# The start of a two-block layer: weight unit 1 in halves, and another order of the first norm's work

## The reference

```python
def rms_norm(x, g):
    y = x * lax.rsqrt(jnp.mean(x * x, axis=-1, keepdims=True) + NORM_EPS)
    return y * g

h = rms_norm(x, norm_mix_g[l])
proj = h @ w_in[l]                       # 1024 -> 5120
q, k, v, c_b, c_c, c_u, g_a, g_b = jnp.split(proj, IN_SPLITS, axis=-1)
q = rms_norm(q.reshape(B, S, SB_HEADS, SB_HEAD_DIM), q_norm_g[l])   # likewise k
branch_a = stick_breaking_attention(q, k, v) @ w_sb_branch[l]
branch_b = short_conv_mixer(c_b, c_c, c_u, conv_w[l]) @ w_conv_branch[l]
merged = jax.nn.sigmoid(g_a) * branch_a + jax.nn.sigmoid(g_b) * branch_b
x = x + merged @ w_out[l]
x = x + hierarchical_moe(rms_norm(x, norm_ffn_g[l]), ...)  # 32 experts
# second block: attention, a gated unit, and a SwiGLU network
```

## Time and profile before

| | before |
|---|---|
| three executions, us | 715.24, 716.45, 718.52 |
| the profiled execution, us | 715.94 |
| its span, first to last instruction, us | 714.1 |
| TensorE busy | 650.1 us, 91% |
| VectorE, ScalarE, GpSimd busy | 47%, 36%, 4% |
| mean granted TensorE clock | 0.959 |
| moved by the transfers | 186.06 MB, mean 261 GB/s |

### The profile page before, as it was taken

One profiled execution on the slowest core, in us unless ns is written; L12 is line 12 of the kernel. 1 busy time (PEld: TensorE's weight loads), 2 busy tenths in 40 slices (PEclk: granted clock), 3 DMA queues, 4 the chain that ended last, 5 costly groups with the idle time before them and its releaser, 6 DMA issues.

```text
span 714.1 us, 11499 instructions
## 1 busy us (share of the span) xinstructions
PE 650.1 (91%) x4957; PEld 530.3 (74%) x4957; DVE 333.6 (47%) x409; ACT 260.5 (36%) x323; POOL 30.4 (4%) x19
## 2 busy tenths in 40 slices
PE   6999999999989999669787899999899999999995
PEld 5789999999856555244432587778689999999994
DVE  5864437566461222001010465759846444444446
ACT  5747454453411111101010453766236443333330
POOL 0610000000100000000000000330000000000000
PEclk9999999999999999957977899999999999999998
DMA  8979334787999999999999998335445556750001
GB/s 316 408 205 357 121 130 167 253 304 262 406 382 406 386 406 408 409 406 406 409 409 407 389 407 315 116 106 189 143 152 177 177 182 191 259 193 0 0 1 60
DMA packets 108491, 186.06 MB, mean 261 GB/s; under 512 B 9632, under 2 KB 33312, under 8 KB 108448
## 3 DMA queue, kind: packets, MB, share of 16 engines
q1 hardware_dynamic: 108160, 185.36, 70.8%
q10 hardware_dynamic: 288, 0.07, 0.0%
HBM read 184.37 MB, written 1.05 MB: 260 GB/s over the span
## 4 chain that ended last, share of the span: by engine, by line
PE 74%; DMA 11%; DVE 10%; ACT 2%; issue 2%; SPq 1%; DVEq 0%; ACTq 0%
PE ps L656 18%; PE ps L658 17%; PE ps L657 17%; PE ps L936 6%; DMA ring<-in_w_up_e 5%; DMA ring<-in_w_down_e 4%; PE ps L956 4%; PE ps L902 3%; DVE w_lo L1767 3%; DMA ring<-in_w_in 1%; PE ps L964 1%; PE ps L966 1%; PE ps L785 1%; ACT w_hi L1303 1%; DVE X L2314 1%
## 5 line engine op out<-in xcount | busy, mean ns | idle before, releaser
L1303 ACT ACTIVATE w_hi<-ring 128x2048 fp32r<-128x2048 f32 (+1 forms) x77 | 141.1, 1859 | 5.4 <-DMA ring<-in_w_in 5.2
L1767 DVE TENSOR_TENSOR w_lo<-ring,w_hi 128x2048 fp32r<-128x2048 f32 x49 | 114.8, 2354 | 52.2 <-ACT w_hi L1303 52.1
L656 PE MATMUL ps<-xT_hi,w_hi 128*128 128x256 f32 x320 | 90.6, 283 | 0.0
L658 PE MATMUL ps<-xT_hi,w_lo 128*128 128x256 f32 x320 | 90.6, 283 | 0.0
L657 PE MATMUL ps<-xT_lo,w_hi 128*128 128x256 f32 x320 | 90.6, 283 | 0.0
L936 PE MATMUL ps<-ring,heT 128*32 128x256 f32 x880 | 59.0, 409 | 15.6 <-DMA ring<-in_w_up_e 11.0
L656 PE MATMUL ps<-hT_hi,w_hi 128*128 128x256 f32 x224 | 64.0, 286 | 0.0
L657 PE MATMUL ps<-hT_lo,w_hi 128*128 128x256 f32 x224 | 63.4, 283 | 0.0
L658 PE MATMUL ps<-hT_hi,w_lo 128*128 128x256 f32 x224 | 63.3, 283 | 0.0
L657 PEld LDWEIGHTS ps<-xT_lo,w_hi 128*128 128x128 f32 x320 | 61.4, 192 | 0.4
L656 PEld LDWEIGHTS ps<-xT_hi,w_hi 128*128 128x128 f32 x320 | 61.4, 192 | 0.4
(11 more groups left out here) (315 smaller groups left out, 1128.5 us busy)
## 6 DMA issues: line engine op xcount, KB each, us to landing
ring<-in_w_in SPq DMA_DIRECT2D x29, 1024.0 KB, 13.7
ring<-in_w_up_e SPq DMA_DIRECT2D x28, 1024.0 KB, 13.4
ring<-in_w_gate_e SPq DMA_DIRECT2D x27, 1024.0 KB, 12.4
ring<-in_w_down_e SPq DMA_DIRECT2D x26, 1024.0 KB, 13.4
ring<-in_w_gate SPq DMA_DIRECT2D x11, 1024.0 KB, 5.4
ring<-in_w_up SPq DMA_DIRECT2D x11, 1024.0 KB, 5.5
ring<-in_w_down SPq DMA_DIRECT2D x11, 1024.0 KB, 5.0
ring<-in_w_out SPq DMA_DIRECT2D x8, 1024.0 KB, 9.8
```

Of the source, the lines that this page charges most:

```text
L656: mm(o, a_hi, b_hi, start=start, stop=False, skip_group_check=True)
L658: return mm(o, a_lo, b_hi, start=False, stop=stop, skip_group_check=True)
L1303: return nc.scalar.activation(o, i, ACT.Copy)
L1767: tt(w_lo[slot][:], ring[:, slot, :], f32(w_hi[:, i % WB, :]), ALU.subtract).then_inc(lo_made, 1)
```

## The change

Five edits are made together. Their names in the diff:

1. Unit 1 is loaded by two transfers of 512 KB, with a semaphore each (`land_w1`, `land[1]`), and split in halves on ScalarE and VectorE (`split_upper(1, j)`, `split_lower(1, j)`). TensorE starts on it when the first lower half is made, and waits for the second at its third step. SyncE issues one more transfer, ahead of the constants and of unit 2.
2. The norm's gain gets its own semaphore (`land_g1`). TensorE's first transposes wait for the identity matrix and x alone.
3. ScalarE splits unit 2 (`hi(2)`) ahead of the second token tile's statistics; VectorE's `lo(2)` stands ahead of the second `refine`, so ahead of `diag`.
4. `first_norm_row` stands between the two token tiles of unit 2, and no longer between units 1 and 2.
5. ScalarE's squares for K come ahead of `hi(4)` and of the copy to `y1_row`, which is now inside `qk_square(0)`, behind `hi(4)`. VectorE's `lo(4)` stands inside `qk_norm(0)`, between the reduction and the small steps.

```diff
@@ SyncE
                 if i >= RING:
                     sp.wait_ge(unit_used, i - RING + 1)
-                if i > 0:
+                if i == 1:
+                    for j in range(2):
+                        sp.dma_start(ring[:, 1, :].rearrange("p (k n) -> p k n", k=KU)[:, 2 * j:2 * j + 2, :],
+                                     src[:, 2 * j:2 * j + 2, :]).then_inc((land_w1, land[1])[j], 16)
+                if i > 1:
                     sp.dma_start(ring[:, slot, :].rearrange("p (k n) -> p k n", k=KU), src).then_inc(land[slot], 16)
@@ TensorE
-                pe.wait_ge(*((part_lo, 1) if i == 0 else (lo_made, i + 1)))
+                pe.wait_ge(*((part_lo, i + 1) if i < 2 else (lo_made, i + 1)))
...
-                        if (i, t, kk) == (0, 0, 2):
-                            pe.wait_ge(lo_made, 1)
+                        if i < 2 and (t, kk) == (0, 2):
+                            pe.wait_ge(lo_made, i + 1)
...
-            pe.wait_ge(land_id, 16 * 2)
+            pe.wait_ge(land_id, 16)
...
-                               (split_made, SP_H + 2 * i + 1, SP_H + 2 * i + 2) if i < 2 else None)
+                               (split_made, SP_H + 2 * i + 1, SP_H + 2 * i + 2) if i < 2 else None,
+                               first_norm_row if i == 2 else None)
...
             proj(1, False)
-            first_norm_row()
             proj(2, False)
@@ ScalarE
-            act.dma_start(g1, norm_mix_g[0].rearrange("(p k) -> p k", k=KD)).then_inc(land_id, 16)
+            act.dma_start(g1, norm_mix_g[0].rearrange("(p k) -> p k", k=KD)).then_inc(land_g1, 16)
...
-            first_unit(0)
+            split_upper(0, 0)
             hR_copy(0)
-            first_unit(1)
+            split_upper(0, 1)
             hR_copy(2)
-            hi(1)
+            split_upper(1, 0)
+            split_upper(1, 1)
             hR_copy(1)
             first_stats(0)
             hR_copy(3)
+            hi(2)
             first_stats(1)
...
-            hi(2)
-
-            def qk_square(which):
+
+            def qk_square(which, between=None):
...
                 last.then_inc(qk_sq, 1)
+                if between:
+                    between()
                 act.wait_ge(qk_ss, which + 1)
...
+            def norm_row():
+                hi(4)
+                act.wait_ge(y1_ps, 1)
+                copy(y1_row[:].rearrange("p t n -> p (t n)"), ps[:, 7, 0:SEQ]).then_inc(y1_copied, 1)
+
             hi(3)
-            act.wait_ge(y1_ps, 1)
-            copy(y1_row[:].rearrange("p t n -> p (t n)"), ps[:, 7, 0:SEQ]).then_inc(y1_copied, 1)
             act.wait_ge(y1_made, 1)
-            qk_square(0)
-            hi(4)
+            qk_square(0, norm_row)
@@ VectorE
             h_scaled(1)
-            lo(1)
+            split_lower(1, 0)
             h_lower(1)
+            split_lower(1, 1)
             h_scaled(3)
             refine(y1[:, 0:1], ss1[:, 0:1], D, RMS_EPS)
             h_lower(3)
+            lo(2)
             refine(y1[:, 1:2], ss1[:, 1:2], D, RMS_EPS)
+            dve.wait_ge(land_id, 16)
...
-            lo(2)
-
-            def qk_norm(which):
+
+            def qk_norm(which, between=None):
...
                 red(ss, sq[:].rearrange("p t (h d) -> p (t h) d", d=HD), AX, ALU.add).then_inc(qk_ss, 1)
+                if between is not None:
+                    lo(between)
                 refine(y, ss, HD, RMS_EPS)
...
             lo(3)
-            qk_norm(0)
-            lo(4)
+            qk_norm(0, 4)
             lo(5)
```

More of the change, by code:

```diff
@@ L258, in build @@
         HALF_OUT = 4
-        PART_S1 = 1
+        PART_S1 = 2
         PS_H, PS_R, PS_X2, PS_G, PS_X3 = 0, 4, 8, 12, 16
@@ L265, in build @@
         land_w0 = sem("land_w0")
+        land_w1 = sem("land_w1")
+        land_g1 = sem("land_g1")
         y1_made = sem("y1_made")
@@ L728, in _, with first_norm_row @@
                 transposes(X, 4, [], (t,))
+            def first_norm_row():
+                pe.wait_ge(land_cst, 16)
+                pe.wait_ge(y1_made, 1)
+                for t in range(T):
+                    last = mm(ps[:, 7, t * P:(t + 1) * P], ones, diag[:, t, :], start=(t == 0), stop=(t == T - 1),
+                              skip_group_check=True)
+                last.then_inc(y1_ps, 1)
             def proj(i, feature):
@@ L736, in proj @@
                     token_unit(i, i // 2, KU * (i % 2), hR_hi, hR_lo, i % 2 == 0, i % 2 == 1,
-                               (split_made, SP_H + 2 * i + 1, SP_H + 2 * i + 2) if i < 2 else None)
-            def first_norm_row():
-                pe.wait_ge(land_cst, 16)
-                pe.wait_ge(y1_made, 1)
-                for t in range(T):
-                    last = mm(ps[:, 7, t * P:(t + 1) * P], ones, diag[:, t, :], start=(t == 0), stop=(t == T - 1),
-                              skip_group_check=True)
-                last.then_inc(y1_ps, 1)
+                               (split_made, SP_H + 2 * i + 1, SP_H + 2 * i + 2) if i < 2 else None,
+                               first_norm_row if i == 2 else None)
             def head_transposes(which):
@@ L1333, in first_stats, with split_upper @@
                 rsqrt(y1[:, t:t + 1], ss1[:, t:t + 1], D, RMS_EPS)
-            def first_unit(j):
+            def split_upper(i, j):
                 part = slice(j * UNIT // 2, (j + 1) * UNIT // 2)
-                act.wait_ge((land_w0, land[0])[j], 16)
-                copy(w_hi[:, 0, part], ring[:, 0, part]).then_inc((part_hi, hi_made)[j], 1)
+                act.wait_ge(land[i] if j else (land_w0, land_w1)[i], 16)
+                copy(w_hi[:, i, part], ring[:, i, part]).then_inc((part_hi, hi_made)[j], 1)
             def normed_copy(b):
@@ L1770, in bc @@
                 return ap.unsqueeze(2).to_broadcast([ap.shape[0], ap.shape[1], n])
-            dve.wait_ge(land_id, 16 * 2)
+            dve.wait_ge(land_g1, 16)
             def scaled(b, base, g, bank):
@@ L1794, in h_lower, with split_lower @@
                 lower_split(b, 4 * (b % 2), b // 2, SP_H + H_ORDER.index(b) - b, hR_hi, hR_lo)
-            def first_unit(j):
+            def split_lower(i, j):
                 part = slice(j * UNIT // 2, (j + 1) * UNIT // 2)
-                dve.wait_ge((part_hi, hi_made)[j], 1)
-                tt(w_lo[0][:, part], ring[:, 0, part], f32(w_hi[:, 0, part]), ALU.subtract
+                dve.wait_ge((part_hi, hi_made)[j], i + 1)
+                tt(w_lo[i][:, part], ring[:, i, part], f32(w_hi[:, i, part]), ALU.subtract
                    ).then_inc((part_lo, lo_made)[j], 1)
             h_scaled(0)
-            first_unit(0)
+            split_lower(0, 0)
             h_lower(0)
             h_scaled(2)
-            first_unit(1)
+            split_lower(0, 1)
             h_lower(2)
             h_scaled(1)
-            lo(1)
+            split_lower(1, 0)
             h_lower(1)
+            split_lower(1, 1)
             h_scaled(3)
```

## The result

The changed kernel takes 719.07 us (median of 20 runs, 716.49 to 722.05), the kernel before in the same runs 716.78 (713.73 to 719.03). The ratio is 1.004, with a 95% interval of 1.0025 to 1.0055: slower by 1.8 to 3.9 us. The ratio itself is within the 0.5% that the prediction called no change; the upper end of its interval is not. The forecast was 719.0, with a range of 715.0 to 721.0. The profiled execution took 720.34 us, of which 718.6 are its span.

A forecast was written before the change was run, and what follows sets the result against it. TensorE was taken to bound the kernel, whose time moves one for one with unit 4's start. A later start (+1.0) and a low clock (+1.5) gave +2.5 us: 719.0 us against a median of 716.45, range 715.0 to 721.0.

The forecast's parts named there:

- The turns: In K's norm, `lo(4)` and five small VectorE steps alternate with GpSimd instructions of 1.29 us; `qk` at 37.5.
- The open point: Whether lines 1760 and 1761 of K's norm also wait for GpSimd: 0.2 us each or 1.29; 1.29 was taken.
- The pause: Ahead of `head_transposes(0)` TensorE waits 4.4 us for VectorE's `qk`, in place of 3.3 us in three places.
- The term that this gave: Unit 4 starts on TensorE at 38.6, after transposes of 1.04 us: 1.0 us later than before.
- The clock: TensorE's clock falls in the long wait before the head transposes; 1.5 us taken, from the program's start.
- The sum: Start of unit 4 and the kernel's end: +1.0 for the later start, +1.5 for the clock, +2.5 us.
- costed at nothing: The gain's own semaphore: first transposes about 1 us earlier, but x's second tile holds the next; no gain.
- it costs nothing: The norm row between unit 2's tiles takes 0.60 us either way, with `y1` ready by 22.7, ahead of 24.4.
- A: Clock stays up through TensorE's wait or returns with the first transposes: +1.0, 717.5 us; chance 0.17.
- B: VectorE goes first at 26.5 or a small step slips past GpSimd, saving 1.2 us: 716.2 or 717.7; chance 0.22.
- C: Clock stays low until behind unit 4, over ten of its matmuls 0.42 us apart: +6.5, 723.0 us; chance 0.08.
- D: Small steps hardly meet a late GpSimd, `qk` is ready by 33, 3.3 us of waits gone: 713.1; chance 0.08.

The follow-up runs named there:

- e2: The changed kernel with one wait more: GpSimd starts only when `qk` of K is made; ratio 0.9993 to the kernel before.
- e7: The changed kernel with the older order of K's norm on ScalarE and VectorE, the other four edits kept; ratio 1.0065 to the kernel before.
- e3: The changed kernel with 16 unused matmuls more on TensorE between unit 3 and the head transposes; ratio 1.0011 to the kernel before.
- e6: The kernel before with only the new order of K's norm on ScalarE and VectorE; 718.07 us, ratio 1.0031 to the kernel before.
- e1: The changed kernel with `lo(4)` back behind K's norm on VectorE; 717.97 us, ratio 1.0034 to the kernel before.
- e4: The changed kernel with GpSimd waiting for K's `qk`, `hi(5)` and `hi(6)` ahead of block copies, `lo(6)` ahead of Q's norm; 715.19 us, ratio 0.9978.
- e8: e1 with 9 unused matmuls more on TensorE behind the first head transposes; ratio 1.0009 to the kernel before.

## Why the prediction was right

**The turns.** This mechanism was as forecast, and its sum right to 0.2 us: GpSimd's start (26.4, measured 26.46), `lo(4)` ready at 26.5 (26.54) and second in turn, `qk` at 37.5 (37.3). The open point was whether lines 1760 and 1761 wait too. They do, for 1.22 and 1.19 us, and e2 and e7 show that it is GpSimd that they wait for. The rows of before could not have shown it. The Trainium skill ("SBUF — State Buffer", "Who interferes with whom") has it that a VectorE instruction with two SBUF inputs and a GpSimd instruction that reads SBUF get in each other's way. The trace agrees, with 1.22 and 1.19 us against 0.17 in the earlier trace rows. Two small slips in the sum offset each other: GpSimd's second instruction, behind a `lo(4)` that ends at 29.9, ends at 31.2 and not at 31.05, and the steps then follow each other every 1.25 us and not every 1.3.

**The pause.** Forecast 4.4 us, measured 4.00: TensorE was free at 33.37 (forecast 33.2), and the transposes began 0.2 us earlier than forecast. The term that this gave, +1.0 us on unit 4, was too large. It adds the transposes' whole 1.04 us, but the next matmul starts before they have ended: 0.85 us behind their start in e3 (37.17 to 38.02). At a full clock the start of the changed kernel would be 0.6 us late (estimate: 37.37 and e3's 11.85 make 49.22, against 48.58).

**The clock.** The fall was forecast, its price in this execution was not: 1.5 us in the sum, 2.5 in the profile (14.37 against e3's 11.85). The row that the term was taken from, the program's start, holds fewer matmuls at the low clock (four of unit 0; here nine of unit 4). The price varies between executions: 1.55 us in e6, with four such matmuls as in that row, and 1.6 in e1's third execution (12.61 us from unit 4 to the mark, against 10.97 in its first), but 2.8 in e7, with fourteen. So 1.5 was a fair value for one execution and too low for this one.

**The sum.** Of its two terms the first was too large (1.0, measured 0.6) and the second too small (1.5, measured 2.5). Their errors offset each other in part: in the profile the start loses 3.16 us, where the sum had 2.5. Over 20 runs the loss is 2.3 us (medians) to 2.9 (ratio). Whether it is smaller than 3.16 because not every execution pays 2.5 us for the clock is not shown, as only one was profiled. That 719.0 meets 719.07 to 0.1 us is luck: the median of the kernel before moved by 0.3 us from 3 runs to 20, and single executions of the changed kernel lie between 716.49 and 722.05.

**Edit 2** was costed at nothing. It starts the first transposes 0.9 us earlier (4.76), but the second ones still wait for x, now behind an idle 1.34 us, and the matmuls of unit 0 reach 0.23 us apart one microsecond later than before. Unit 0 ended 0.35 us later. It is hidden by the pause that follows. Whether edit 2 or only a later x in this execution (8.07 against 7.93) made it so, no run of edit 2 alone shows.

**Edits 1, 3 and 4** took away the waits that they were said to take away. What stands on the other side was in the sum as well, but "it costs nothing" for edit 4 holds only with edit 5, as e7 indicates.

**The rivals.** A (full clock) did not occur in the profiled execution of the changed kernel, though e1 shows that shorter pauses do pass with a full clock. B did not occur; GpSimd was first both here and in e6, by 0.08 us here. C did not occur, but it was near: the clock was back within unit 4, after nine matmuls, where C began at over ten, and e7 had fourteen. D was refuted by the starts.

## What to carry to other kernels

When VectorE's small steps stand beside a GpSimd sequence without gaps, each costs one GpSimd instruction (here 1.25 us instead of 0.2); count them, and hold GpSimd back until the waited-for result is out, if its own has time. Three short waits of TensorE can be cheaper than a long one, which costs the clock too, and one profile does not tell how often it does. So before moving work ahead, look at what then stands in front of the next result that TensorE waits for.

## What the runs showed of the hardware

The granted clock fell in or behind pauses of TensorE of 2.40, 2.46 and 4.00 us (e2, e6, the changed kernel), behind a pair of 1.46 and 2.32 us (e7), and behind one pair of 0.82 and 2.33 us in one execution of three (e1). It stayed up behind one of 2.12 us (e4). All but e1 are one execution each, so a length from which it falls can't be read from them. It can fall after the engine has resumed: in e2 TensorE was at work again at 41.90, and the clock was 1.00 up to 43 and 0.50 from 44 on. Sixteen matmuls put into the pause of 4.00 us (e3) kept it up in the profiled execution. With nine in e1's second pause (e8) it was up too, but so it was in two of e1's three executions without them.

Single executions of one kernel on one chip spread over 710.75 to 719.72 us (35 runs of the kernel before). In the profiles most of this spread lies behind 200 us: in the three executions of e1 the part ahead of it differs by 2.4 us and the part behind it by 7.1, and over all kernels the part behind it took 509.7 to 517.4 us. The mean granted clock from 290 to 400 us, among the experts, lay between 0.76 and 0.84; whether that makes the whole spread was not tried. Twelve runs here gave intervals of 0.19 to 0.26% to either side, 1.3 to 1.9 us. The mark in the trace repeats to 0.5 us where the clock stays up (48.36 and 47.91 in e1), and not where it falls (50.30).
